# A two-layer hybrid decoder trunk on one core: the output projection's first weights split one stage earlier, and the rows of the result turned and stored from within the last MLP

## What is computed

```
x = x + concat([o_nsa, o_hg]) @ w_out[l]
h2 = rms_norm(x, mlp_norm_g[l])
x = x + square(relu(h2 @ w_up[l])) @ w_down[l]
```

## Time and profile before

| | |
|---|---|
| Median of 3 runs | 2060.67 us (2057.65 to 2062.05) |
| Profiled execution's own time | 2054.93 us |
| Span in its profile | 2053.1 us |
| PE busy | 1905.8 us (93%) |
| DVE, ACT, POOL busy | 1138.6, 828.1, 692.3 us |
| Mean granted clock | 0.966 |

### The profile page before, as it was taken

One profiled execution on the slowest core, in us unless ns is written; L12 is line 12 of the kernel. 1 busy time (PEld: TensorE's weight loads), 2 busy tenths in 40 slices (PEclk: granted clock), 3 DMA queues, 4 the chain that ended last, 5 costly groups with the idle time before them and its releaser, 6 DMA issues. The chain is left out here.

```text
span 2053.1 us, 38910 instructions
## 1 busy us (share of the span) xinstructions
PE 1905.8 (93%) x15789; PEld 1785.9 (87%) x15789; DVE 1138.6 (55%) x1899; ACT 828.1 (40%) x1809; POOL 692.3 (34%) x470
## 2 busy tenths in 40 slices
PE   6999798988799999999999997989887999999998
PEld 6999555988599999999999984668875999999998
DVE  4589655454455555555528886555535454545454
ACT  4594355353534131313146923544435341313130
POOL 2325435240043333333323542443201333333331
PEclk8999888999999999999999997999999999999999
DMA  4220520432522222222222223222254222222221
GB/s 155 86 80 23 164 66 9 117 93 70 158 83 83 83 83 84 82 87 83 78 85 84 63 73 104 58 64 67 83 154 111 83 71 93 78 92 81 85 82 48
DMA packets 200638, 175.80 MB, mean 86 GB/s; under 512 B 11356, under 2 KB 198030, under 8 KB 200334
## 3 DMA queue, kind: packets, MB, share of 16 engines
q1 hardware_dynamic: 200354, 173.30, 27.7%
q10 hardware_dynamic: 108, 0.03, 0.0%
HBM read 162.67 MB, written 10.62 MB: 84 GB/s over the span
## 5 line engine op out<-in xcount | busy, mean ns | idle before, releaser
L427 POOL TENSOR_TENSOR WX<-RAW,WX 128x2048 fp32r<-128x2048 f32 (+2 forms) x48 | 222.4, 4634 | 523.0 <-ACT WX L423 523.0
L2391 DVE TENSOR_TENSOR sq<-sq 128x288 f32<-128x288 f32 x128 | 156.9, 1231 | 196.8 <-ACT sq L2360 196.8
L427 POOL TENSOR_TENSOR m_wl<-RAW,m_wh 128x2048 fp32r<-128x2048 f32 x36 | 166.5, 4624 | 285.1 <-ACT m_wh L423 285.1
L439 PE MATMUL bank<-UH,m_wl 128*128 128x288 f32 x640 | 188.7, 295 | 0.0
L438 PE MATMUL bank<-UL,m_wh 128*128 128x288 f32 x640 | 188.7, 295 | 0.0
L437 PE MATMUL bank<-UH,m_wh 128*128 128x288 f32 x640 | 188.6, 295 | 0.0
L439 PE MATMUL bank<-UH,WX 128*128 128x288 f32 x576 | 170.0, 295 | 0.0
L438 PE MATMUL bank<-UL,WX 128*128 128x288 f32 x576 | 169.8, 295 | 0.0
L437 PE MATMUL bank<-UH,WX 128*128 128x288 f32 x576 | 169.6, 295 | 0.0
L2410 DVE TENSOR_TENSOR OT<-bank,rstd 128x288 f32<-128x288 f32 x128 | 58.2, 455 | 183.2 <-PE bank L439 183.2
L2413 DVE TENSOR_TENSOR XT<-XT,OT 128x288 f32<-128x288 f32 x128 | 156.3, 1221 | 4.4
(11 more groups left out here) (386 smaller groups left out, 5829.3 us busy)
## 6 DMA issues: line engine op xcount, KB each, us to landing
RAW<-in_w_up SPq DMA_DIRECT2D x32, 1024.0 KB, 5.4
RAW<-in_w_down SPq DMA_DIRECT2D x32, 1024.0 KB, 5.2
RAW<-in_w_in SPq DMA_DIRECT2D x20, 1024.0 KB, 5.3
R<-in_cache_nsa_kv SPq DMA_DIRECT2D x128, 64.0 KB
HT<-in_cache_nsa_kv SPq DMA_DIRECT2D x128, 64.0 KB, 2.6
RAW<-in_w_in SPq DMA_DIRECT2D x6, 1056.0 KB, 5.4
R<-in_cache_nsa_kv SPq DMA_DIRECT2D x48, 128.0 KB, 2.8
out<-R SPq DMA_DIRECT2D x10, 512.0 KB, 5.0
```

What stands on the lines that cost most here:

```text
L427: eng.tensor_tensor(S.granule(S.wl, i, w)[:, chunks], S.granule(S.raw, i, w)[:, chunks], S.granule(S.wh, i, w)[:, chunks].bitcast(F32), AL ...
L439: ins = pe.matmul(out, wl[:, c, cols], ah[:, c, n], start=False, stop=(c == KC - 1))
L2391: dve.tensor_tensor(relu[n % 4], relu[n % 4], relu[n % 4], ALU.mult).then_inc(sem("relu_squared"), 1)
```

## The change

The ring of the past has six places and a list, `PLACE`, says who takes which: sample 6 takes the place of sample 0, and sample 7 that of sample 2. Sample 5's load waits for `s_valued`, sample 6's for `b_valued` 1, sample 7's for `b_valued` 2, with the load of the projection's granule 0 between the last two and that of granule 1 behind them. Within the samples' block ACT splits granule 0 after its work for pair 2, and POOL makes the low part; the MLP's block then starts with granule 0 ready (`ready` is 1 in place of 0).

In the last layer's MLP the last four down granules are interleaved with `turn_prompt` (4 transposes of one chunk, kept by ACT and stored by SP as soon as a group of chunks is there); the samples' 8 transposes come at the end, kept by DVE. The clearing of semaphores after the last layer and the block behind it are gone. The core of the diff:

```
-            RING = 7
+
+            PLACE = (0, 1, 2, 3, 4, 5, 0, 2)
...
             def past_count(b):
-                return 16 * (NPG + 1) * (b // RING + 1)
+                return 16 * (NPG + 1) * (PLACE[:b].count(PLACE[b]) + 1)
...
             cmp_scope.close()
+            open_wx()
             smp_scope = ExitStack()
-            R2 = smp_scope.enter_context(nc.sbuf_tensor(f"R2s_{l}", [P, R2_N], F32))
-            KTS = smp_scope.enter_context(nc.sbuf_tensor(f"KTS_{l}", [P, SLOT], F32, side="right"))
-
-            slots += [(R2, 0, R2, 2048), (R2, 3072, R2, 5120), (R1, 0, R1, 2048)]
-            assert len(slots) == RING
+            R2 = smp_scope.enter_context(nc.sbuf_tensor(f"R2s_{l}", [P, 3072 + 14 * P], F32))
+            KTS = smp_scope.enter_context(nc.sbuf_tensor(f"KTS_{l}", [P, 3072], F32, side="right"))
+
+            slots += [(R2, 0, R2, 2048), (R1, 0, R1, 2048)]
+            assert len(slots) == max(PLACE) + 1
...
                 def _(sp):
-                    for b in range(4, NB):
-                        if b == RING - 1:
-
-                            sp.wait_ge(sem("s_valued"), 1)
-                        if b >= RING:
-                            sp.wait_ge(sem("b_valued"), (b - RING) // 2 + 1)
-                        load_past(sp, b)
-
-                    sp.wait_ge(sem("b_valued"), 2)
+                    load_past(sp, 4)
+
+                    sp.wait_ge(sem("s_valued"), 1)
+                    load_past(sp, 5)
+                    sp.wait_ge(sem("b_valued"), 1)
+                    load_past(sp, 6)
+
                     for g in range(2):
                         load_out_granule(sp, RAW[:, g * KC * GWX:g * KC * GWX + KC * GW].rearrange("p (c n) -> p c n", c=KC), g,
                                          sem(f"m_w_raw{g}"))
+                        if g == 0:
+                            sp.wait_ge(sem("b_valued"), 2)
+                            load_past(sp, 7)
+
+                @block.gpsimd
+                def _(pool):
+
+                    pool.wait_ge(sem("out_hi"), 1)
+                    pool.tensor_tensor(w0_part(1), W0, w0_part(0).bitcast(F32), ALU.subtract)
...
                             act.activation(dst, src, ACT.Copy).then_inc(sem("pT_kept"), 1)
+                        if a == 2:
+                            act.wait_ge(sem("m_w_raw0"), 16 * 3)
+                            act.activation(w0_part(0), W0, ACT.Copy).then_inc(sem("out_hi"), 1)
...
-            open_wx()
             mlp_scope = ExitStack()
             S7 = Split(mlp_scope, "m_", l, [sem(f"m_w_raw{i}") for i in range(2)],
-                       lambda i: i // 2 + 1 + 2 * min(i // 2 + 1, 2), 0)
+                       lambda i: i // 2 + 1 + 2 * min(i // 2 + 1, 2), 1)
...
+            last = l + 1 == DEPTH
+            if last:
+                Y = mlp_scope.enter_context(nc.sbuf_tensor("Y", [P, NT * DM], F32))[:, :].rearrange("p (t c) -> p t c", t=NT)
+                YS = mlp_scope.enter_context(nc.sbuf_tensor("YS", [P, DM], F32))[0:NS, :]
...
-                        if i == 2:
-                            sp.wait_ge(sem("m_first_lo"), 1)
                         if kind == "out":
                             if i >= 2:
-                                sp.wait_ge(sem("m_w_lo"), i - 1)
+                                if i >= 3:
+                                    sp.wait_ge(sem("m_w_lo"), i - 2)
...
+                    if last:
+                        for a, b in ((0, 4), (4, 6), (6, 7), (7, 8)):
+                            sp.wait_ge(sem("y_kept"), b)
+                            sp.dma_start(y_prompt[0, :, a * P:b * P].rearrange("(t p) c -> p t c", p=P), Y[:, :, a * P:b * P]
+                                         ).then_inc(sem("y_stored"), 16)
+                        sp.wait_ge(sem("ys_kept"), 1)
+                        sp.dma_start(y_sample.rearrange("b t c -> (b t) c"), YS).then_inc(sem("y_stored"), 16)
+                        sp.wait_ge(sem("y_stored"), 16 * 5)
...
-                    for i in range(len(G7)):
-                        split_lo(pool, S7, i, GW, slice(0 if i else KC // 2, KC))
+                    for i in range(1, len(G7)):
+                        split_lo(pool, S7, i, GW)
...
-                    pe.wait_ge(sem("m_first_lo"), 1)
-                    first_products(pe, bank[2:6], S7, 0, GW, "mix_lo", lambda c: c + 1, "m_w_lo", (UH, UL))
+                    def turn_prompt(c):
+                        pe.wait_ge(sem("m_grown"), 16 * 3 + 2 * c + 2)
+                        if c >= 2:
+                            pe.wait_ge(sem("y_kept"), c - 1)
+                        for t in range(NT):
+                            ins = pe.transpose(bank[c % 2][:, t * P:(t + 1) * P], XT[:, c, t * P:(t + 1) * P], ident)
+                        ins.then_inc(sem("y_turned"), 1)
+
+                    def turn_samples(c):
+                        b = bank[2 + (len(U7) + c // 4) % 6]
+                        return pe.transpose(b[0:NS, c % 4 * P:(c % 4 + 1) * P], XT[:, c, SEQ:N], ident)
+
+                    first_products(pe, bank[2:6], S7, 0, GW, "mix_lo", lambda c: c + 1, (UH, UL))
...
+                        if last and kind == "down" and q == 3 and s == 1 and m >= 1:
+                            turn_prompt(m - 1)
+                    if last:
+
+                        pe.wait_ge(sem("m_added"), RANK[-5])
+                        for c in range(KC - 1):
+                            turn_samples(c)
+                        turn_prompt(KC - 1)
+                        turn_samples(KC - 1).then_inc(sem("ys_turned"), 1)
...
-                    split_hi(act, S7, 0, GW, 0)
+                    def keep_prompt(c):
+                        act.wait_ge(sem("y_turned"), c + 1)
+                        act.activation(Y[:, :, c * P:(c + 1) * P], bank[c % 2].rearrange("p (t n) -> p t n", t=NT), ACT.Copy
+                                       ).then_inc(sem("y_kept"), 1)
+
...
+                        if last and kind == "down" and q == 3 and s == 1 and m >= 1:
+                            keep_prompt(m - 1)
...
+                    if last:
+                        keep_prompt(KC - 1)
...
-                    split_lo(dve, S7, 0, GW, slice(0, KC // 2), "first_lo")
...
+                    if last:
+                        dve.wait_ge(sem("ys_turned"), 1)
+                        for i in range(2):
+                            ins = dve.tensor_copy(YS[:, i * 512:(i + 1) * 512], bank[2 + (len(U7) + i) % 6][0:NS, :])
+                        ins.then_inc(sem("ys_kept"), 1)
...
-        YU = [(t, q) for t in range(TT) for q in range(2)]
-        xout = [ctx.enter_context(nc.sbuf_tensor(f"xout{i}", [P, SLOT], F32)) for i in range(2)]
-        Y = [xout[0][:, :].rearrange("p (t c) -> p t c", t=NT), xout[1][:, 0:DM].rearrange("p (t c) -> p t c", t=1)]
-        with nc.Block() as block:
-            @block.tensor
...
```

More of the change, by code:

```diff
@@ L423, in split_hi, with split_lo @@
             act.activation(S.granule(S.wh, i, w), S.granule(S.raw, i, w), ACT.Copy).then_inc(sem(S.name + "w_hi"), 1)
-        def split_lo(eng, S, i, w, chunks=slice(0, KC), name="w_lo"):
+        def split_lo(eng, S, i, w):
             eng.wait_ge(sem(S.name + "w_hi"), i + 1 - S.ready)
-            eng.tensor_tensor(S.granule(S.wl, i, w)[:, chunks], S.granule(S.raw, i, w)[:, chunks],
-                              S.granule(S.wh, i, w)[:, chunks].bitcast(F32), ALU.subtract).then_inc(sem(S.name + name), 1)
+            eng.tensor_tensor(S.granule(S.wl, i, w), S.granule(S.raw, i, w), S.granule(S.wh, i, w).bitcast(F32), ALU.subtract
+                              ).then_inc(sem(S.name + "w_lo"), 1)
         def feature_product(pe, out, S, i, w, cols, ah, al, n, operand=None):
@@ L444, in keep_warm, with first_products @@
             pe.matmul(out[:, 0:n], ident, cst[:, 0:n], start=True, stop=True)
-        def first_products(pe, banks, S, i, w, done, counts, second_half=None, operand=None):
+        def first_products(pe, banks, S, i, w, done, counts, operand=None):
             wh, wl = S.granule(S.wh, i, w), S.granule(S.wl, i, w)
@@ L2052, in layer @@
             Sb = [cut(1664) for _ in range(2)]
-            cut = cutter(R2, 6144)
+            cut = cutter(R2, 3072)
             PT = cut(14 * P).rearrange("p (j r) -> p j r", j=14)
@@ L2294, in _ @@
                         load_granule(sp, S7, i, src)
-                    if l + 1 < DEPTH:
+                    if last:
[6 more added lines that the diff above has]
+                        sp.wait_ge(sem("y_stored"), 16 * 5)
+                    else:
                         for i in range(2):
-                            sp.wait_ge(sem("m_w_lo"), len(G7) - 1 + i)
+                            sp.wait_ge(sem("m_w_lo"), len(G7) - 2 + i)
                             load_first_projection(sp, l + 1, i)
@@ L2413, in _ @@
                                 dve.tensor_tensor(x, x, grown[n % 2], ALU.add).then_inc(sem("m_grown"), 1)
+                    if last:
```

(34 more changed lines are left out.)

16 lines of the change are left out of this document (7 added, 9 removed).

## The result

The changed kernel takes 2072.28 us (median of five runs, 2070.22 to 2074.67) where the kernel before, timed beside it, takes 2060.67. The ratio is 1.0058, with a 95% interval of 1.0043 to 1.0074: 11.6 us slower, of which 8.9 to 15.2 can be told. The forecast was 7.9 slower, 2068.6 in a range of 2061 to 2075.

What follows compares the result with a forecast made beforehand. TensorE, busy 93% of the span, was taken as the bound, with no slack in the samples' block. The terms -9.3 + 2.0 + 16.0 + 3.0 - 3.8 = +7.9 us on 2060.67 gave 2068.6 us, range 2061 to 2075.

Steps and rivals of the forecast that it cites:

- What bounds the kernel: Whole kernel: TensorE busy 93% of the span; samples' block a chain over PE, ACT and DVE without slack.
- Part 1: Output projection's start: granule 0 split early lets PE start 4.65 us sooner a layer, -9.3 us in all.
- Part 2: Samples' block: ACT's copy moved ahead of pair 3's exponentials costs 1.0 us a layer, +2.0 us in all.
- Part 3, the stall: Samples' block, ring of six: PE stands 8.0 us a layer waiting for sample 7's load, +16.0 us in all.
- The upper bound of 9.0: Stall ahead of sample 7's transposes: 9.0 us if the tail of granule 0 delays the load.
- The lower bound of 6.3: Stall ahead of sample 7's transposes: 6.3 us if all of the load lands at the pace of issue.
- Part 3, the clock: Behind the stall: TensorE returns at the lower clock, 1.5 us a layer (bounds 0 and 3), +3.0 us in all.
- Part 4: Kernel's end: last product 2.9 us later, but idle time and most copies and stores behind it go, -3.8 us.
- The sum: Whole kernel: all terms together +7.9 us, giving a median of 2068.6 us; chance 0.70.
- Clock and transfer both kind: Rival, samples' block and projection: load lands at issue pace, clock costs little; -0.5 us, 2060.2; chance 0.12.
- No stall: Rival, sample 7's transposes: PE gets there late anyway and the load is covered; -11.1 us, 2049.6; chance 0.06.
- Heavier: Rival, stall and end: clock back late (3.0 a layer), narrow stores end last; +13.2 us, 2073.9; chance 0.12.

Runs made afterwards that it cites:

- the wait alone: Kernel before, ring of seven kept, with sample 7's load waiting for pair 1's values instead of pair 0's: 2084.5 us, ratio 1.0112.
- the kernel with a seventh place: Kernel after, plus a seventh place for a sample's cache pieced together from unused R1 and RAW, granule 1 loaded after pair 3's values: 2048.34 us, ratio 0.9942.
- The quiet run: Kernel before with sample 7's load waiting for pair 1's values and the projection's granules held back so nothing else is on the queues: 2081.31 us, ratio 1.0094.
- Filling the stall: Kernel after with ten idle products of 512 columns on PE ahead of its wait for sample 7: 2066.08 us, ratio 1.0027.
- the end alone: Kernel before with only the new rows, stores and transposes of the last MLP, no change to front or ring: 2057.39 us, ratio 0.9977.
- idle products: Kernel after with a seventh cache place, plus three 512-column products nobody reads around PE's wait ahead of the projection: 2044.59 us, ratio 0.9926.
- the kernel with sample 7 in RAW: Kernel after, but sample 7 takes sample 1's place, granule 0 loads after pair 1's values, granule 1 after pair 3's: 2058.78 us, ratio 0.9992.

## Where the prediction was right and where not, point by point

- **What bounds the kernel.** Right where a run tells: the wait alone moved the total by its stall and the low clock behind it, and the kernel with a seventh place by what its trace had less of (11.5 expected, 11.2 to 11.9 measured).
- **Part 1, -9.3.** Right. PE's wait ahead of the projection is 2.7 us in both layers, 4.6 less each, and the kernel with a seventh place returns it in the total.
- **Part 2, +2.0.** Right, a little high: the new wait on ACT ahead of pair 3's probabilities is 0.7 us, and with what stands behind it 0.9 a layer, 1.8. VectorE was held by GpSimd's subtraction, as the row of 5.16 suggested. DVE and POOL, kernel after:

```profile
571.62 2.45 DVE L2234 TENSOR_TENSOR HT<-HT 128x2 f32<-128x2 f32 x1
...
569.53 4.52 POOL L2090 TENSOR_TENSOR WX<-RAW,WX 128x2048 fp32r<-128x2048 f32 x1 [88.66 <-ACT WX L2204]
```

  A multiply of two columns takes 2.45 us, in place of 0.16 for the median of its kind, and ends at 574.07, with the POOL instruction (569.53 + 4.52 = 574.05). Its result is used later, so it costs nothing, as said.
- **Part 3, the stall, +16.0.** The mechanism was right, in its place and its cause; this is one of two terms that were mis-sized. It measured 9.77 and 8.94 us, 18.7 in both layers. The step that failed is that of the duration: I took issue (4.01) and landing (4.4) of the same load from a moment when nothing followed it on the queue for 7 us. The upper bound of 9.0 had granule 0 in front of the load but left out granule 1 behind it, and was too low for layer 0. The quiet run has PE waiting for 7.5 and the wait alone for 8.8 and 8.5, with the transfer behind. The slower issue, 1.0 and 0.6 us, is the other part, and its cause is open. (The lower bound of 6.3 is 6.2 by its own rows.)
- **Part 3, the clock, +3.0.** The other one: 3.45 and 3.73 us, 7.2 in both layers, outside even my bound of 3 a layer. The clock stayed low for 8.3 and 8.9 us, through all transposes and nearly all scores, and it is the scores, 2.4 and 2.6 us longer, that cost most of it. Filling the stall took 6.2 to 6.4 us back out. What failed is a reading: I took layer 1's rows for a clock that comes back some 4 us after PE resumes. PE had resumed earlier. In that trace (kernel before) the line ahead of the earlier trace rows, and the stretches around the rise, are:

```profile
1517.73 1.94 PE L1641 MATMUL bank<-R 128*128 128x64 f32 x8 [6.06 <-DVE R L1875]
...
1523.50:1524.00 0.50, 0.50 (x5) 0.50 (x4) 0.00 (x0) 0.25 (x1) 0.00 (x0) 0.50 0.72 207
1524.00:1524.50 0.50, 0.50 (x5) 0.50 (x4) 0.00 (x0) 0.50 (x1) 0.00 (x0) 0.72 0.88 285
```

  So there was a wait of 6.06 us (5.8 in layer 0, which the account of PE's waits in the prediction passes over, as it lies just ahead of the block), then eight products, then the transposes, and the clock rose near 1524.3, 6.6 us after PE resumed. With 6.6 us in place of 4 the same sum gives an estimate of 2.6 us a layer (1.1 up to the scores, and half of the 3.1 us by which the low stretch reaches into them): nearer to 3.5 and 3.7, and still short of them.

  The rule of the Trainium skill (TensorE: Matmul & The Clock Gate, "Part 4: PE-mode transpose") that I set aside says that transposes don't count as work for the clock. The row I held against it is weaker than I wrote, since eight products stand before its transposes. The end of the kernel before is the plain case against the rule: after the last product, at 2039.81, PE makes nothing but its 40 transposes, from 2042.19 on; the clock falls near 2043.1 and comes back in their midst:

```profile
2043.30:2046.50 3.20, 3.20 (x17) 3.20 (x16) 2.85 (x5) 0.00 (x0) 0.00 (x0) 0.50 0.40 164
2046.50:2048.40 1.90, 1.90 (x17) 1.64 (x15) 1.76 (x4) 0.00 (x0) 0.00 (x0) 1.00 0.76 308
```

  The stretch behind the stall decides nothing about the rule: its transposes last 2.8 us, and the low clock outlives 4.8 us of score products as well.
- **Part 4, -3.8.** Right: the trace gives 2.7 us of transposes ahead of the last product (from 24 in the way of the last MLP) against 6.75 us less behind it, -4.0; the end alone measured -3.5 to -4.7. The narrow stores, which no row priced, end ahead of the samples' store: hidden, as taken.
- **The sum.** -9.2 + 1.8 + 18.7 + 7.2 - 4.0 = +14.5 us by the trace, against +7.9; the two terms of part 3 carry the whole difference. By that sum the time would have been 2075.2, just beyond the upper end of the forecast range. The medians say +11.6, with 15.2 as the upper end; what makes them smaller than the trace's sum no run shows, so that the result lies well inside the range is in part luck. The wait alone by its ratio, with the front, the copies and the end as they measured, gives 23.1 - 9.2 + 1.8 - 4.0 = 11.7.
- **The rivals.** Clock and transfer both kind: wrong, both were harsher. No stall: shown wrong by the wait itself, and shown right in its price once the stall was taken out, at -11.9 against its -11.1. Heavier: this is half of what came, with its late clock (3.0 a layer, measured 3.5 and 3.7), but not its narrow stores; at +13.2 it is nearer to the medians (1.6 off) than the forecast (3.7 off).

## What to carry to other kernels

A place taken from a ring costs what its last user's distance to the next reader leaves exposed of the whole load: read from the timeline when the values end, when the transposes begin, and how long the load takes from the first issue to the last landing, in the company it will have on the queue after the change, not the one it has now. Price a stall on TensorE at its length plus the work behind it at half the clock, here for 8 to 9 us, and count a row's time to the full clock from where TensorE really resumed. And where a short wait of TensorE's can't be removed, idle products that end as it ends can keep the clock up at no cost: 1.4 and 1.3 us in the two layers here.

## What was not expected of the hardware

- The time to the full clock after PE resumes varies in this kernel: 8.3 and 8.9 us after the stalls of 9.6 and 8.8, 6.6 after the waits of 5.8 and 6.1 ahead of the samples' block, 3.6 at the projection behind a wait of 2.7 in the kernel with a seventh place (567.61 to 571.2), 6.0 behind a wait of 2.7 in the kernel with sample 7 in RAW. What sets it is left open.
- In the kernel after, the projection starts at full clock and drops 0.85 us later, while PE is busy. Its stretches, columns as above:

```profile
580.25:581.10 0.85, 0.85 (x6) 0.85 (x7) 0.85 (x2) 0.85 (x3) 0.00 (x0) 1.00 0.84 269
581.10:584.50 3.40, 3.40 (x16) 3.40 (x15) 3.40 (x6) 3.40 (x6) 0.00 (x0) 0.50 0.93 232
```

  So the smaller wait did not spare the projection its low stretch of 3.4 us, it only began later.
- A load's landing time depends on what is issued right behind it: sample 7's window of 512 KB lands in 4.1 us with quiet queues and 4.4 in the kernel before (7 us of quiet behind it), and in 4.7 to 5.4 in the kernel after and the wait alone, with 1 or 2 MB of weights behind it.
- Executions differ by some us in stretches that no edit touches: from the start of the last low part of layer 0's projection to layer 1's samples' block it is 896.2 us in the kernel before, 897.0 in the kernel after, 899.7 in the end alone and 900.1 in the wait alone. The profiled execution of the kernel before is 5.7 us under its median. A difference of spans (17.4 us here) was half again the difference of the medians (11.6).
